# A hybrid conformer block on 8 cores: 24 of 33 token tiles transposed by DMA in place of TensorE, and adaLN gates later in the convolution stage

## The chip, the cores and the metric

One Trainium2 chip, 8 cores. Each core runs the same program on its own 2,048 tokens (and 32 tokens of halo before them); nothing is exchanged between cores. The time is the device time of the slowest core, in microseconds. The profile is of one execution, on its slowest core (core 4).

## The reference

```python
mod = silu(c) @ w_ada + b_ada                        # six vectors of 1024: shift, scale, gate, twice
h = layernorm(x) * (1 + scale1) + shift1             # (16384, 1024)
z = h @ w_in + b_in                                  # 7168 columns, split in seven
a_val, a_gate, b_gb, b_gc, b_x, g_a, g_b = split(z)
u = a_val * sigmoid(a_gate)
u = causal_depthwise_conv(u, conv_a_w, 31) + conv_a_b
u = silu(layernorm(u, ln_a_g, ln_a_b))
y_a = u @ w_a_out + b_a_out
y_b = (b_gb * causal_depthwise_conv(b_gc * b_x, conv_b_w, 3)) @ w_b_out
merged = sigmoid(g_a) * y_a + sigmoid(g_b) * y_b
x = layernorm(alpha * x + (1 + gate1) * (merged @ w_o + b_o), ln1_g, ln1_b)
h = layernorm(x) * (1 + scale2) + shift2
f = square(relu(h @ w_up + b_up))                    # 4096 columns
x = layernorm(alpha * x + (1 + gate2) * (f @ w_down + b_down), ln2_g, ln2_b)
```

Inputs and outputs are f32; the kernel multiplies in bf16.

## The kernel before

A core works on two blocks (`b` = 0, 1) of 1,024 tokens, each eight tiles of 128 tokens (`NT` = 8). Matmuls want channels on the partitions, x arrives with tokens on them. So each token tile is normalised with tokens on the partitions (`xn`, `h2n`, bf16, 128x1024), then transposed in eight 128x128 pieces into `hT` (the input of w_in) or `h2T` (the input of w_up), where the modulation `* (1 + scale) + shift` has one scalar per partition. There are 33 such tiles: the halo tile and eight of block 0's h, eight of block 1's h, and eight of h2 in each block.

The stages follow one another on TensorE: h and GLU of block 0; convolution stage of block 0 (24 steps `n_` in `token_mix`; each does a pair of projections for p, the first 16 also a piece of the 31-wide convolution); the B gate (16 steps); the merge (32 steps of two groups of eight 512-column matmuls); then GLU, convolution, gate and merge of block 1; up-projection of block 0 (64 steps of eight matmuls), down-projection, and both for block 1.

Work on other tiles is laid between these steps. `Plan` is a table from step to calls: `plan.add(n, fn, i)`; `plan.run(n)` makes them after step n. In block 0's merge it prepares block 1's h (`p1_setup`: `load`, `stats`, `root`, `norm`, `trans`). In block 1's merge it does block 0's output projection and both layer norms (`p3_setup`: `bias`, `proj`, `root1`, `ln1`, `root2`, `ln0`, `trans`), and in the up-projection of block 0 the same for block 1. The order of the calls is the order of the instructions on each engine's queue; there is no other scheduler.

`transpose_evac` does a transpose: eight TensorE transposes against an identity into banks 6 and 7 of PSUM (line 531), then one instruction per piece that applies the modulation while it reads PSUM, some on ScalarE (line 558), the rest on VectorE (line 550): four and four for block 1's h, five and three for h2. Block 0's h is transposed raw (lines 536 and 538) and modulated in place later, by `modulate` (lines 776 and 780). Matmuls rotate over the other six banks (`brot`).

`hT` has room for the halo in each of eight runs (`PW` = 132 columns, of which `NPH` = 128 are the tile's), in block 1 too; there the matmuls read `[4][128]` or `[3][128]` columns out of runs of 132 (`hcols`, `cols`).

DMAs that load weights are issued by GpSimd (they cast f32 to bf16), through a ring of four 1 MB slots (`ws_get`, `ws_release`); SP issues the loads of x, the relays of u, the stores of x1 (`ln1`) and the output. An engine waits at the head of its queue, in order.

The vectors of `mod` come from w_ada in twelve tiles of 512 columns. Tiles 4 and 5 (gate1), 6 and 7 (shift2), 8 and 9 (scale2), and 10 and 11 (gate2) are loaded two at a time into a place that two tiles share; each pair is used by 64 one-column matmuls (`ada_cols`), and only then is the next loaded. `xc0_side(n)` does this in the convolution stage of block 0: gate1 after step 2, its row (`ada_rows`, TensorE, then a DMA to `gd`) after step 3, its spread to all partitions as `g1b` after step 8, shift2 after 11, scale2 after 20. `gb0_side` uses tiles 10 and 11 after step 11 of the next stage.

Of the kernel before, what the change touches and what calls it, by code (L numbers as in the profile page):

```python
# [251 lines left out]
def build_program(needed=None):  # L252
# [1280 lines left out]
```

How the kernel before makes its waits and increments, by code:

```python
    def wait_ev(self, ev, same_ok=False):  # L63
        if ev is None:
            return
        sem, val, key = ev
        if key == self.name and (same_ok or not self.selfsync):
            return
        sid = id(sem)
        if self.seen.get(sid, 0) >= val:
            return
        self.h.wait_ge(sem, self.fw.sem_value(key, val))
        self.seen[sid] = val
# [14 lines left out]
    def mark(self, inst, reads=(), writes=()):  # L88
        self.idx += 1
        if self.fw.needs_inc(self.name, self.idx):
            self.cnt += 1
            inst.then_inc(self.sem, 1)
        ev = (self.sem, self.idx, self.name)
        for r in reads:
            r.r[self.name] = ev
        for w in writes:
            w.w = ev
            w.r = {}
        return ev
# [7 lines left out]
    def dma(self, out, in_, owner, reads=(), writes=()):  # L107
        self.deps(reads, writes)
        if owner.dsem is None:
            self.fw.nsem += 1
            owner.dsem = self.fw.nc.alloc_semaphore("d%d_%s" % (self.fw.nsem, owner.name))
        owner.dcnt += 16
        inst = self.h.dma_start(out=out, in_=in_)
        inst.then_inc(owner.dsem, 16)
        ev = (owner.dsem, owner.dcnt, "dma_" + owner.name)
        for r in reads:
            r.r["dma_%s_%d" % (owner.name, owner.dcnt)] = ev
        for w in writes:
            w.w = ev
            w.r = {}
        return ev
```

## Time and profile before

| | us |
|---|---|
| time, median of 3 runs (1172.16 to 1173.83) | 1172.42 |
| the profiled execution, its own time | 1171.64 |
| its span, slowest core; all cores 1164.0 to 1170.6 | 1170.6 |
| TensorE busy | 1100.7 |
| VectorE busy | 677.6 |
| ScalarE busy | 437.1 |
| GpSimd busy | 175.2 |

Busy times are of instructions; those of TensorE overlap at their ends, and a 512-column matmul that is listed with 379 ns follows the one before it after some 216 ns. The granted clock of TensorE is given as a share of full speed.

### The profile page before, as it was taken

To read this page: it belongs to the slowest core of one execution; us is meant where nothing else is said; L and a number is where in the kernel's file an instruction comes from. 1 tells how busy PE (TensorE), PEld (TensorE's weight loads), DVE (VectorE), ACT (ScalarE), POOL (GpSimd) and SP (SyncE) were. 2 spreads that over 40 slices of the span, in tenths; PEclk is the share of its full clock that TensorE was granted. 3 is DMA by queue.
4 is the path that set the end of the run, shared out by engine and by line. 5 is a ranking of instruction groups with operands and counts; after the bars stand their busy time and mean duration, and the time that the engine had idled before them with its cause. 6 is when DMAs were issued, how large, how long until landed. Compare 5 with 4: busy or idle time off the path is not lost.

```text
span 1170.6 us, 19292 instructions; the slowest of 8 cores (1164.0 to 1170.6 us)
## 1 busy us (share of the span) xinstructions
PE 1100.7 (94%) x6607; PEld 578.1 (49%) x6676; DVE 677.6 (58%) x1159; ACT 437.1 (37%) x773; POOL 175.2 (15%) x159
## 2 busy tenths in 40 slices
PE   1699899999999999999999999999999999999994
PEld 1366577444445677644444444444444444444441
DVE  4538576847653267588877767877032782210567
ACT  2344334844442234584466644456000043320000
POOL 4004011102100000111321021210060000004200
PEclk9999899999999999999999999999999999999998
DMA  9999959998645652398764584636944399644412
GB/s 185 180 142 124 162 90 146 166 229 169 77 73 92 111 90 35 59 180 162 127 129 92 123 157 109 130 73 141 220 72 72 73 203 240 97 73 72 73 54 90
DMA packets 150335, 143.14 MB, mean 122 GB/s; under 512 B 33840, under 2 KB 138688, under 8 KB 149984
## 3 DMA queue, kind: packets, MB, share of 16 engines
q0 software_dynamic: 106736, 87.73, 52.7%
q1 hardware_dynamic: 43504, 54.18, 16.5%
q8 instruction: 55, 0.90, 0.3%
q14 instruction: 40, 0.33, 0.1%
HBM read 203.22 MB, written 16.79 MB: 188 GB/s over the span
## 4 chain that ended last, share of the span: by engine, by line
PE 79%; DVE 8%; DMA 5%; issue 4%; ACT 3%; POOL 1%; DVEq 0%; ACTq 0%; POOLq 0%; SPq 0%
PE bank L161 78%; DMA wb<-w_in 4%; ACT nb L1063 2%; DMA wada<-w_ada 2%; DVE cbuf L1055 1%; DVE slot L500 1%; PE bank L531 1%; DVE x1r L515 1%; DVE x1r L1256 0%; DVE gt L1254 0%; DVE fT L1236 0%; ACT sg L1135 0%; DVE sg L1138 0%; DVE dg L1083 0%; DVE x L664 0%
## 5 line engine op out<-in xcount | busy, mean ns | idle before, releaser
L161 PE MATMUL bank<-hT,wb 128*128 128x512 bf16 (+4 forms) x2112 | 388.8, 337 | 1.9 <-ACT sg L1135 1.3
L161 PEld LDWEIGHTS bank<-hT,wb 128*128 128x128 bf16 x2112 | 202.7, 98 | 157.2 <-issue 14.4
L161 PE MATMUL bank<-h2T,wb 128*128 128x512 bf16 x1002 | 222.8, 379 | 3.1 <-DVE x L664 1.9
L161 PE MATMUL bank<-wb,fT 128*128 128x512 bf16 x1004 | 220.3, 379 | 1.1
L161 PEld LDWEIGHTS bank<-wb,fT 128*128 128x128 bf16 x1024 | 100.2, 98 | 120.8
L161 PEld LDWEIGHTS bank<-h2T,wb 128*128 128x128 bf16 x1024 | 99.8, 98 | 121.3 <-issue 2.9
L1234 ACT ACTIVATE rr<-bank,pvec 128x512 bf16<-128x512 f32 x128 | 85.1, 683 | 111.0 <-PE bank L161 108.9
L1236 DVE TENSOR_TENSOR fT<-rr 128x512 bf16<-128x512 bf16 x128 | 63.4, 513 | 91.0 <-ACT rr L1234 90.9
L505 ACT ACTIVATE slot<-slot,eps 128x1 f32<-128x1 f32 (+1 forms) x65 | 17.6, 291 | 253.1 <-DVE slot L502 239.1
L1254 DVE TENSOR_TENSOR gt<-bank,g2b 128x512 f32<-128x512 f32 x32 | 21.8, 682 | 121.9 <-PE bank L161 121.9
L138 POOL DMA_DIRECT2D wb<-w_in x40 | 36.3, 938 | 316.9 <-PE bank L161 296.2
L1181 ACT ACTIVATE sg<-bank,pvec 128x512 f32<-128x512 f32 x64 | 43.5, 683 | 80.1 <-PE bank L161 72.2
L903 ACT ACTIVATE sg<-bank,pvec 128x384 f32<-128x384 f32 (+3 forms) x84 | 45.3, 539 | 72.7 <-PE bank L161 69.7
L1063 ACT ACTIVATE nb<-cbuf,pvec 128x128 bf16<-128x128 f32 x128 | 63.0, 492 | 11.5 <-DVE cbuf L1055 1.3
L161 PE MATMUL bank<-v,wb 128*128 128x512 bf16 x244 | 58.8, 379 | 1.1 <-DVE v L1152 0.5
L161 PE MATMUL bank<-u,wb 128*128 128x512 bf16 x246 | 58.8, 379 | 0.5
L161 PE MATMUL bank<-wo,merged 128*128 128x512 bf16 x251 | 57.6, 379 | 0.3
L910 DVE SCALAR_TENSOR_TENSOR p<-bank,pvec,sg 128x396 bf16<-128x396 f32 (+3 forms) x48 | 27.8, 578 | 45.1 <-PE bank L161 28.7
L500 DVE BATCH_NORM_STATS2 slot<-x 128x6 f32<-128x512 f32 x64 | 44.4, 694 | 7.0 <-DVE x L517 0.5
L138 POOL DMA_DIRECT2D wb<-w_up x16 | 14.2, 890 | 223.1 <-PE bank L161 179.5
L910 DVE SCALAR_TENSOR_TENSOR u<-bank,pvec,sg 128x384 bf16<-128x384 f32 (+3 forms) x36 | 20.8, 577 | 46.3 <-PE bank L161 41.8
L997 DVE TENSOR_TENSOR wt<-wtab,cmask 128x2560 bf16<-128x2560 bf16 x32 | 47.3, 1482 | 0.0
(113 smaller groups left out, 1135.4 us busy)
## 6 DMA issues: line engine op xcount, KB each, us to landing
wb<-w_in POOLq DMA_DIRECT2D x16, 1024.0 KB, 14.3
wb<-w_up POOLq DMA_DIRECT2D x16, 1024.0 KB, 11.8
wb<-w_down POOLq DMA_DIRECT2D x16, 1024.0 KB, 8.2
wada<-w_ada POOLq DMA_DIRECT2D x12, 1024.0 KB, 18.6
wb<-w_in POOLq DMA_DIRECT2D x24, 512.0 KB, 16.6
xt<-xs SPq DMA_DIRECT2D x16, 512.0 KB, 10.0
x<-xs SPq DMA_DIRECT2D x16, 512.0 KB, 5.7
x1d<-x SPq DMA_DIRECT2D x16, 512.0 KB, 3.4
```

The lines of the kernel that those rows point to most:

```text
L138: inst = eng.h.dma_start(out=out, in_=in_)
L161: inst = pe.h.matmul(out, lhsT, rhs, start=self.first, stop=last)
L500: dve.op(lambda e: e.bn_stats(st[:npart, hh, :], src[:npart, hh * 512:(hh + 1) * 512]), reads=[rsrc, res], writes=[res])
L505: act.op(lambda e: e.activation(sl["sd"][:npart, :], sl["mv"][:npart, 1:2], AF.Sqrt, bias=eps_ap[:npart, :], scale=1.0), reads=[sl["res"], ...
L903: act.op(lambda e: e.activation(sg[k][:, 0:n], bank_ap[bi][:, 0:n], func, bias=pvec[:, PV_BIN + ca + j:PV_BIN + ca + 1 + j], scale=1.0), r ...
L910: dve.op(lambda e: e.scalar_tensor_tensor(cols(dst, j), view(bank_ap[bi2]), pvec[:, PV_BIN + cb + j:PV_BIN + cb + 1 + j], view(sg[k]), ALU ...
L997: dve.op(lambda e: e.tensor_tensor(t.rearrange("p a m (c q) -> p (a m) c q", q=R), tab, msk, ALU.mult), reads=[r_wtab, r_cmask], writes=[r ...
L1063: act.op(lambda e: e.activation(nb[:, s_, :], cbuf[:, jb, s_, :], AF.Silu, bias=pvec[:, PV_LAB + gi:PV_LAB + gi + 1], scale=pvec[:, PV_LAG ...
L1181: act.op(lambda e: e.activation(sg[k], bank_ap[bi], AF.Sigmoid, bias=pvec[:, bcol:bcol + 1], scale=1.0), reads=[bank_res[bi], r_pvec], wri ...
L1234: act.op(lambda e: e.activation(rr[k], bank_ap[bi], AF.Relu, bias=pvec[:, PV_BUP + fc:PV_BUP + fc + 1], scale=1.0), reads=[bank_res[bi], r ...
L1236: dve.op(lambda e: e.tensor_tensor(fT[:, fc, s * 512:(s + 1) * 512], rr[k], rr[k], ALU.mult), reads=[r_rr[k]], writes=[r_fT[fc][s]])
L1254: dve.op(lambda e: e.tensor_tensor(gt[t % 2], bank_ap[t], g2b[:, hs], ALU.mult), reads=[bank_res[t], r_g2], writes=[r_gt[t % 2]])
```

## The change

- `p1_setup` of block 1 and `p3_setup` of both blocks: `trans` no longer calls `transpose_evac`, but `dma_transpose`, one DMA from SP for the whole tile, from `xn` or `h2n` into `hT` or `h2T`. It waits on SP for the normalised tile and signals its own semaphore.
- The modulation is a call of its own, `mod`, over a group of tiles: three (the last time two) for block 1's h, two for h2; in place, channels chunks 0 to 4 on VectorE and 5 to 7 on ScalarE. It is planned two to four steps behind the group's last transpose.
- Block 1's `hT` is laid out without room for the halo, 1,024 columns, and its matmuls read and write contiguous columns.
- The first of the eight groups of the up-projection goes over the first 512 tokens for all four column pieces, then over the other 512.
- `xc0_side`: gate1 after step 7 (was 2), its row after 8 (3), its spread after 12 (8), shift2 after 14 (11), scale2 after 22 (20); the loads of w_ada that follow each move with them.

```diff
+    def modulate_tiles(hT, r_hT, t0, t1, sc, sh, rm):
+        for kc in range(KC):
+            view = hT[:, kc, t0 * 128:t1 * 128]
+            x_ = 0 if kc < 5 else 1
+            rw = [r_hT[t][x_] for t in range(t0, t1)]
+            if kc < 5:
+                dve.op(lambda e: e.tensor_scalar(view, view, modT[:, sc + kc:sc + kc + 1], modT[:, sh + kc:sh + kc + 1], ALU.mult, ALU.add),
+                       reads=rw + [rm], writes=rw)
+            else:
+                act.op(lambda e: e.activation(view, view, AF.Identity, bias=modT[:, sh + kc:sh + kc + 1], scale=modT[:, sc + kc:sc + kc + 1]),
+                       reads=rw + [rm], writes=rw)
+
+    def dma_transpose(dst, src, owner, reads, writes):
+        sp.deps(reads, writes)
...
+        owner.dcnt += 16
+        sp.h.dma_start(out=dst, in_=src, transpose=True).then_inc(owner.dsem, 16)
...
     def p1_setup(b, ring, xn_offs, raw, n_dve):
-        hT = sb(OFF_H[b], [128, KC, TW], BF16, "hT")
+        hT = sb(OFF_H[b], [128, KC, TW if raw else TB], BF16, "hT")
...
         def trans(i):
             npart, ri, dv = tiles[i]
+            if not raw:
+                dma_transpose(hT[:, :, i * 128:(i + 1) * 128], xn[i % nxn], own("tr%d" % (i % nxn)), [r_xn[i % nxn]], r_hT[ri])
+                return
             transpose_evac(xn[i % nxn], npart, r_xn[i % nxn], hT, r_hT[ri], dv, None if raw else (SC1, SH1, r_mod1), n_dve)
+        def mod(g):
+            modulate_tiles(hT, r_hT[1:], 3 * g, min(3 * g + 3, NT), SC1, SH1, r_mod1)
...
         def trans(t):
-            transpose_evac(h2n[t % 2], 128, r_h2n[t % 2], h2T, r_h2T[t], lambda dst, kc: dst[:, kc, t * 128:(t + 1) * 128],
-                           (SC2, SH2, r_mod2), n_dve)
+            dma_transpose(h2T[:, :, t * 128:(t + 1) * 128], h2n[t % 2], own("tr2_%d" % (t % 2)), [r_h2n[t % 2]], r_h2T[t])
+
+        def mod(i):
+            modulate_tiles(h2T, r_h2T, 2 * i, 2 * i + 2, SC2, SH2, r_mod2)
...
         def hcols(kc, s):
+            if b > 0:
+                return hT[:, kc, s * 512:(s + 1) * 512]
             return hT[:, kc, :].rearrange("p (r n) -> p r n", n=PW)[:, 4 * s:4 * s + 4, PW - NPH:PW]
...
-            for jj in range(4):
+            for jj, s in ([(jj, s) for s in range(NS) for jj in range(4)] if g == 0 else [(jj, s) for jj in range(4) for s in range(NS)]):
...
     def xc0_side(n):
-        if n == 2:
+        if n == 7:
             ada_gate(0)
-        if n == 3:
+        if n == 8:
             ada_rows(0)
-        if n == 8:
+        if n == 12:
             ada_spread(0)
-        if n in (11, 20):
-            nts, c_ = ((6, 7), SH2) if n == 11 else ((8, 9), SC2)
+        if n in (14, 22):
+            nts, c_ = ((6, 7), SH2) if n == 14 else ((8, 9), SC2)
...
-        if n in (2, 11, 20):
-            n0 = {2: 6, 11: 8, 20: 10}[n]
+        if n in (7, 14, 22):
+            n0 = {7: 6, 14: 8, 22: 10}[n]
...
-                    plan.add(9 * g + 8 + 2 * i, pp["trans"], t)
+                    plan.add(9 * g + 7 + 2 * i, pp["trans"], t)
...
+            plan.add(min(9 * g + 14, 30), pp["mod"], g)
...
-        p3_plan(pp, 2, 3, (1, 2, 4, 5, 7))
+        p3_plan(pp, 2, 3, (1, 2, 4, 5, 6), 2, 31)
...
+            if t % 2 == 1:
+                plan.add(min(n + lags[4] + mlag, last), pp["mod"], t // 2)
...
-    p3_plan(H2[1], 4, 6, (2, 4, 7, 9, 13))
+    p3_plan(H2[1], 4, 6, (2, 4, 7, 9, 11), 4, 63)
```

## Rows read from the trace of the kernel before

**Rows 1.** The page, busy time by engine (share of the span), xinstructions.
```profile
PE 1100.7 (94%) x6607; PEld 578.1 (49%) x6676; DVE 677.6 (58%) x1159; ACT 437.1 (37%) x773; POOL 175.2 (15%) x159
```
**Rows 2.** Windows by stage: window, length, busy PE PEld DVE ACT POOL, PEclk, DMA share, GB/s.
```profile
262.00:374.00 112.00, 111.53 (x579) 54.40 (x586) 62.06 (x114) 45.50 (x79) 15.48 (x14) 1.00 0.66 109
567.00:677.00 110.00, 109.42 (x548) 51.54 (x558) 85.35 (x151) 66.78 (x103) 18.74 (x14) 1.00 0.61 122
677.00:790.00 113.00, 110.53 (x534) 51.30 (x543) 84.20 (x145) 50.36 (x91) 22.42 (x14) 1.00 0.55 117
822.00:1113.00 291.00, 289.63 (x1323) 131.87 (x1348) 100.49 (x170) 46.57 (x73) 51.73 (x37) 1.00 0.64 117
```
**Rows 3.** The page, chain that ended last, share of the span by engine.
```profile
PE 79%; DVE 8%; DMA 5%; issue 4%; ACT 3%; POOL 1%; DVEq 0%; ACTq 0%; POOLq 0%; SPq 0%
```
**Rows 4.** Timeline of TensorE in block 0's merge: start, us, operation.
```profile
285.38 0.61 PE L531 MATMUL bank<-ident,xn 128*128 128x128 bf16 x8
285.83 1.89 PE L161 MATMUL bank<-hT,wb 128*128 128x512 bf16 x8
287.56 1.89 PE L161 MATMUL bank<-v,wb 128*128 128x512 bf16 x8
289.28 1.89 PE L161 MATMUL bank<-hT,wb 128*128 128x512 bf16 x8
```
**Rows 5.** Timeline of TensorE in block 0's convolution stage, [idle before <-releaser].
```profile
115.57 2.84 PE L161 MATMUL bank<-hT,wb 128*128 128x396 bf16 x16
118.25 1.29 PE L161 MATMUL bank<-ur,wt 128*128 128x128 bf16 x20
...
122.72 0.95 PE L161 MATMUL bank<-cact,wada 128*128 128x1 bf16 x32
129.13 0.99 PE L161 MATMUL bank<-cact,wada 128*128 128x1 bf16 x32 [5.46 <-DMA wada<-w_ada]
129.99 5.37 PE L161 MATMUL bank<-hT,wb 128*128 128x396 bf16 x16
135.20 1.29 PE L161 MATMUL bank<-ur,wt 128*128 128x128 bf16 x20
```
**Rows 6.** Windows around that pause, columns as in rows 2.
```profile
123.70:129.10 5.40, 0.00 (x0) 0.00 (x0) 1.17 (x1) 1.01 (x2) 0.88 (x1) 0.61 1.14 177
129.10:135.30 6.20, 6.17 (x50) 3.37 (x51) 0.34 (x2) 0.59 (x1) 0.87 (x1) 0.51 1.18 179
135.30:150.00 14.70, 14.70 (x151) 10.48 (x149) 11.78 (x17) 6.01 (x12) 0.00 (x0) 1.00 1.16 159
```
**Rows 7.** Timeline of GpSimd, 60 to 300 us: issue of tiles 4 and 5.
```profile
109.93 2.13 POOL L138 DMA_DIRECT2D wada<-w_ada  x2
```
**Rows 8.** DMA issues, 115 to 160 us: count, size, median us to landing.
```profile
wada<-w_ada POOLq DMA_DIRECT2D x2, 1024.0 KB, 26.2
```
**Rows 9.** Groups by form: busy us, mean ns | idle before, releasers.
```profile
L558 ACT ACTIVATE h2T<-bank,modT 128x128 bf16<-128x128 bf16 x80 | 36.6, 457 | 15.5 <-PE bank L531 9.5
L550 DVE TENSOR_SCALAR h2T<-bank,modT 128x128 bf16<-128x128 bf16 x48 | 16.4, 342 | 3.5
L780 ACT ACTIVATE hT<-hT,modT 128x396 bf16<-128x396 bf16 x6 | 4.3, 715 | 2.8 <-DVE modT L463 2.4
L776 DVE TENSOR_SCALAR hT<-hT,modT 128x396 bf16<-128x396 bf16 x10 | 3.8, 382 | 0.9
L776 DVE TENSOR_SCALAR hT<-hT,modT 128x264 bf16<-128x264 bf16 x5 | 1.9, 380 | 0.4
```
**Rows 10.** DMA view, 215 to 260 us: packets, hardware queue, SBUF-to-SBUF copies.
```profile
DMA packets 17565, 8.87 MB, mean 197 GB/s; under 512 B 8909, under 2 KB 16930, under 8 KB 17556
...
q1 hardware_dynamic: 9416, 4.69, 50.4%
...
u<-nb SPq DMA_DIRECT2D x26, 64.0 KB, 8.7
```
**Rows 11.** DMA issues of the whole span: store of one x1 tile.
```profile
x1d<-x SPq DMA_DIRECT2D x16, 512.0 KB, 3.4
```
**Rows 12.** Timeline in the first up-projection: TensorE behind VectorE.
```profile
768.85 3.61 PE L161 MATMUL bank<-h2T,wb 128*128 128x512 bf16 x15 [1.24 <-DVE x L664]
```

More of the change, by code:

```diff
@@ L595, in x_ring @@
         return slot, load
+    def modulate_tiles(hT, r_hT, t0, t1, sc, sh, rm):
[11 more added lines that the diff above has]
+        sp.deps(reads, writes)
+        if owner.dsem is None:
+            fw.nsem += 1
+            owner.dsem = nc.alloc_semaphore("d%d_%s" % (fw.nsem, owner.name))
+        owner.dcnt += 16
+        sp.h.dma_start(out=dst, in_=src, transpose=True).then_inc(owner.dsem, 16)
+        ev = (owner.dsem, owner.dcnt, "dma_" + owner.name)
+        for r in reads:
+            r.r["dma_%s_%d" % (owner.name, owner.dcnt)] = ev
+        for w in writes:
+            w.w = ev
+            w.r = {}
     def p1_setup(b, ring, xn_offs, raw, n_dve):
-        hT = sb(OFF_H[b], [128, KC, TW], BF16, "hT")
+        hT = sb(OFF_H[b], [128, KC, TW if raw else TB], BF16, "hT")
         _g = new_group(fw, ["hT%d_%d%s" % (b, t, ab) for t in range(NT + 1) for ab in "ab"], OFF_H[b], OFF_H[b] + HSZ)
@@ L631, in trans @@
             npart, ri, dv = tiles[i]
+            if not raw:
+                dma_transpose(hT[:, :, i * 128:(i + 1) * 128], xn[i % nxn], own("tr%d" % (i % nxn)), [r_xn[i % nxn]], r_hT[ri])
+                return
             transpose_evac(xn[i % nxn], npart, r_xn[i % nxn], hT, r_hT[ri], dv, None if raw else (SC1, SH1, r_mod1), n_dve)
-        return dict(hT=hT, r_hT=r_hT, load=load, stats=stats, root=root, norm=norm, trans=trans, n=len(tiles))
+        def mod(g):
+            modulate_tiles(hT, r_hT[1:], 3 * g, min(3 * g + 3, NT), SC1, SH1, r_mod1)
+        return dict(hT=hT, r_hT=r_hT, load=load, stats=stats, root=root, norm=norm, trans=trans, mod=mod, n=len(tiles))
     def p3_setup(b, mg, r_mg, wo, x1_offs, h2n_offs, n_dve):
@@ L863, in hcols, with hbank @@
         def hcols(kc, s):
+            if b > 0:
+                return hT[:, kc, s * 512:(s + 1) * 512]
             return hT[:, kc, :].rearrange("p (r n) -> p r n", n=PW)[:, 4 * s:4 * s + 4, PW - NPH:PW]
+        def hbank(ap):
+            return ap if b > 0 else grp4(ap)
         u = sb(OFF_U, [128, KC, TW], BF16, "u")
@@ L896, in view, with hin @@
                     return ap[:, 0:n].rearrange("p (r n) -> p r n", n=NPH)
+            def hin(kc):
+                return cols(hT, kc) if b == 0 else hT[:, kc, r0_ * 128:r1_ * 128]
             rd = hT_reads(r0_, r1_, b == 0)
@@ L900, in pair @@
             for kc in range(KC):
-                grp.mm(view(bank_ap[bi]), wa[:, kc, jj * 128:(jj + 1) * 128], cols(hT, kc), [ra[jj // 2]] + rd, last=(kc == KC - 1))
+                grp.mm(bank_ap[bi][:, 0:n], wa[:, kc, jj * 128:(jj + 1) * 128], hin(kc), [ra[jj // 2]] + rd, last=(kc == KC - 1))
             k = sg_rot.next()
@@ L908, in pair @@
             for kc in range(KC):
-                grp.mm(view(bank_ap[bi2]), wb[:, kc, jj * 128:(jj + 1) * 128], cols(hT, kc), [rb[jj // 2]] + rd, last=(kc == KC - 1))
+                grp.mm(bank_ap[bi2][:, 0:n], wb[:, kc, jj * 128:(jj + 1) * 128], hin(kc), [rb[jj // 2]] + rd, last=(kc == KC - 1))
             dve.op(lambda e: e.scalar_tensor_tensor(cols(dst, j), view(bank_ap[bi2]),
@@ L1176, in branch @@
             for kc in range(KC):
-                grp.mm(grp4(bank_ap[bi]), wt_[:, kc, jj * 128:(jj + 1) * 128], hcols(kc, s),
+                grp.mm(hbank(bank_ap[bi]), wt_[:, kc, jj * 128:(jj + 1) * 128], hcols(kc, s),
                        [rt_[0]] + hT_reads(4 * s, 4 * s + 4, False), last=(kc == KC - 1))
@@ L1223, in up @@
             wu, ru, iu = ws_get()
-            for jj in range(4):
+            for jj, s in ([(jj, s) for s in range(NS) for jj in range(4)] if g == 0 else [(jj, s) for jj in range(4) for s in range(NS)]):
                 fc = 4 * g + jj
-                for s in range(NS):
+                if True:
                     bi = brot.next()
@@ L1429, in after_gb1, with p3_plan @@
         plan.add(0, scale_wo, 15)
-        p3_plan(pp, 2, 3, (1, 2, 4, 5, 7))
-    def p3_plan(pp, first, step, lags):
+        p3_plan(pp, 2, 3, (1, 2, 4, 5, 6), 2, 31)
+    def p3_plan(pp, first, step, lags, mlag, last):
         nx = pp["nx1"]
```

4 lines of the change are left out of this document (2 added, 2 removed).

## The prediction

> **What bounds the kernel now.** The page comes first: TensorE is busy 1100.7 us, 94% of the span [rows 1]. The windows by stage come next. In each the reader is to compare TensorE's busy time with the length of the window: 111.53 of 112 us while block 0 merges, 109.42 of 110 while block 1 merges, 110.53 of 113 in the first up-projection, 289.63 of 291 behind it. VectorE reaches 85.35 of 110 and 84.20 of 113 us in the second and third, ScalarE 66.78 and 50.36, the DMA share 0.61 and 0.55 [rows 2]. The chain of waits says the same: 79% of it is TensorE [rows 3]. So in the stages where the 24 tiles are transposed, an instruction taken off TensorE shortens the end by its length, unless something new comes late. One real pause lies outside of them, in the convolution stage of block 0 [rows 5].
>
> **The change, part by part.**
>
> *Transposes leave TensorE.* The timeline shows what one tile costs: its eight transposes start at 285.38 and the next matmul at 285.83, so 0.45 us [rows 4] (the row's 0.61 us is the modelled end of a pipelined group). Sixteen matmuls behind them take 3.45 us (285.83 to 289.28), which is one step of the merge stage. 24 tiles, eight of block 1's h and sixteen of h2, are 24 x 0.445 = **10.7 us** of TensorE. They lie between saturated matmuls, so they are on the path. The 512-column matmuls that read hT and those that read v keep the same pace (1.73 us for eight, by their starts in rows 4), though hT is read there in four strided runs: making it contiguous gains nothing visible, and I cost it at nothing.
>
> *The adaLN gate moves.* At step 2 of the convolution stage TensorE does the first 32 one-column matmuls at 122.72 and then waits 5.46 us for the tile of w_ada [rows 5]. The clock's rows show what follows: granted 0.61 in the wait and 0.51 in the 6.2 us behind it, the lower of the two levels (1.2 GHz), where all else is at 1.00 [rows 6]. Sixteen matmuls of 396 columns take 135.20 - 129.99 = 5.21 us there, against 118.25 - 115.57 = 2.68 at full clock, so 2.5 us more [rows 5]. Moving the gate to step 7 asks for the tile five steps of about 3.9 us later, about 142 in the old timeline without the pause. It landed by 129.1. The wait and its slow clock go: 5.5 + 2.5 = **8.0 us**. Nothing of the moved work itself disappears (the one-column matmuls, the row, its DMA and the spread DMA on SP only run later, and the first user of g1b is bob, behind this stage).
>
> What is late next: three loads of w_ada are issued later too. Tiles 6 and 7 are now asked for at step 7 and used at step 14, seven steps or 27 us; 8 and 9 at step 14 and used at step 22, four steps of some 3.9 us and four shorter ones, about 24 us. A pair issued amid this stage's weight loads took 26.2 us to land, but it stood behind other tiles and the engines were saturated [rows 8]; the pair before was issued at 109.93 and had landed by 129.1, 19 us, and the one for 8 and 9 is issued at about 160 to 170, when the backlog is worked off [rows 7]. Cost from 0 to 3 us; I take nothing, as both covers are above 19 us.
>
> *Modulation in place.* Before, each h2 tile took five ScalarE reads of PSUM of 457 ns and three VectorE ones of 342 ns. After, a pair of tiles takes five VectorE instructions in place and three of ScalarE. The nearest rows are the same operation in place on 396 columns: 382 ns on VectorE, 715 ns on ScalarE, and 380 ns for 264 columns on VectorE [rows 9]. Over the sixteen h2 tiles VectorE goes from 48 x 0.342 = 16.4 us to 8 x 5 x 0.38 = 15.2, ScalarE from 80 x 0.457 = 36.6 to at most 8 x 3 x 0.715 = 17.2. For block 1's h, VectorE has 15 instructions of 0.38 = 5.7 us and ScalarE nine of up to 0.715 = 6.4, both less than the 8 tiles x 4 of before. Neither engine gets more work. Both stand beside TensorE, so this is worth nothing on the path. Whether it costs something depends on the wait it brings.
>
> *The new wait.* Transpose and store both issue from SP; modulation of a group waits for its last transpose at the head of VectorE and ScalarE, and behind it stand the evacuations of the banks that TensorE refills (six banks, three merge steps). Time from the normalised tile to its modulation: in block 0's merge four steps of 3.45 us, 13.8 us. In block 1's merge the transpose of tile t stands on SP behind the store of tile t+1, and two steps (about 4.6 us each with the third of a projection that falls to them) are left, 9.2 us; in the up-projection five steps of 2.3 us, 11.5 us. How long does a DMA transpose of 256 KB take? None is in this trace. From below, a 512 KB store lands in 3.4 us [rows 11]; 3.4 us is less than every cover. From above, the SBUF-to-SBUF copies of u<-nb, in rows of 256 bytes: one of 64 KB lands in 8.7 us behind its seven companions of the group [rows 10]; four of them end to end would be 35 us. As the eight of a group are together 512 KB and land in little more than one, I take 5 to 9 us for a tile. That is at or below all three covers, and a wait of 1 or 2 us is still hidden by the free banks where VectorE has room (62.06 of 112 us in block 0's merge). It has little in the up-projection, where TensorE already loses time to VectorE, as in the 1.24 us before the matmuls at 768.85 [rows 12]: 2.5 us in the window of 113, against 0.5 at the rate of the last window. VectorE's 84.2 us would then stand against 109.4 us and no longer 113. Of the eight transposes taken out there (3.6 us) I give half back, **1.8 us**; the bounds are 0 and the whole 3.6 plus the present 2 again.
>
> The order of the first up-projection group (all of one half of the tokens first) gives the last pair four groups of eight matmuls, 4 x 1.73 = 6.9 us more. No cost.
>
> *Load on the DMA engines.* 24 transposes of 256 KB. In the window with u<-nb the hardware queue's 9,416 packets took 50.4% of 16 engines over 45 us [rows 10], 38.5 ns each; 1,024 rows of 256 bytes are 39 us of one engine, or 2.5 us of all sixteen for each tile. Free are 34% of 112 us (38), 39% of 110 (43) and 45% of 113 (51) [rows 2], for eight tiles each: 4.8, 5.4 and 6.4 us a tile. So weights stay on time, at no cost. The bounds are 0 and the second rival's.
>
> The Trainium skill (VectorE: DVE Perf Modes, The three transpose paths) speaks against the change: it gives 1309 ns for a 128x128 transpose by DMA against 390 on TensorE, and advises TensorE where PSUM will do. By it a tile of eight blocks, if they run one after another, would be an estimated 10.5 us, which would lead to the first rival below; the trace shows TensorE at 0.45 us for all eight, and no DMA transpose.
>
> **Sum.** The profiled execution took 1171.6 us (span 1170.6). 1171.6 - 10.7 - 8.0 + 1.8 = 1154.7. The median of the runs, 1172.4, lies 0.8 above that execution, so **1155.5 us**.
>
> **Rivals.**
>
> *The DMA lands behind its cover* and gives the transposes' gain back: a tile takes 12 to 15 us, modulation holds VectorE, and TensorE waits for banks. For it: the 9.2 us cover and the order on SP. Against it: 8.7 us for the copies [rows 10]. Price: of 16 h2 tiles in 8 groups, each late by about 4 us with 2.5 absorbed, 8 x 1.5 = 12; so about 1164 to 1167.
>
> *The transposes fill the DMA engines* and the weights come late: slower than before. For it: the engines are 55 to 66% taken [rows 2] and the real size of a transpose's pieces isn't known. If a tile goes in pieces of 64 bytes at the same 38.5 ns, it holds all engines for 4,096 x 38.5 / 16 = 9.9 us, so eight need 79. Block 0's merge then needs 0.66 x 112 + 79 = 153 us of 112, block 1's 146 of 110, the up-projection 141 of 113: 41, 36 and 28 us too many. Three weight tiles loaded ahead, each 64 matmuls or 13.8 us long, hide 41 us in the first stage and once in the two adjacent ones: 36 + 28 - 41 = 23 us remain. With the lower clock after such pauses, as after the one at 129, two or three times 2.5: 1155.5 + 23 + 7 = 1185. It decides from about 9 us of all engines per tile on (where it costs the 17 us won). Against it: rows of 256 bytes would need only 2.5. This is also the case in which the DMA does not do what the change asks of it.
>
> *The pause only moves* to step 14 or 22 because w_ada tiles are asked for later: 8.0 us not won, 1163.5. For it: the landing of 26.2 us [rows 8] against a cover of about 24. Against it: the queue is shorter when they are issued.
>
> **How the numbers follow.** Forecast 0.62 (its own range 1151 to 1160: no give-back below, 3.6 + 2 above, and the same spread as the runs). DMA behind its cover 0.13, pause moves 0.09, DMA engines full 0.16. The range 1149 to 1170 holds the first, the third and most of the second. Changes under 0.2% (2.3 us) could not be told from none here. Faster: 0.62 + 0.09 + most of 0.13 = 0.81; same 0.04; slower 0.15.
>
> **What would show it.** Right: no 5.46 us idle for w_ada and a clock of 1.00 between 123 and 135; TensorE's matmuls fewer by 192; DMA transposes that land in 5 to 9 us; in the three stages TensorE still busy to within 1% and the windows shorter by 3.6 us each. Wrong: VectorE or ScalarE waiting for the transposing DMA, with TensorE waiting for them; a DMA share near 1 in the merge stages and TensorE waiting for wb; a new wait for w_ada at step 14 or 22; the up-projection as long as before.

## The result: slower, 1188.6 us

The changed kernel took 1188.55 us (median; the kernel before on the same chip 1172.45). Its time over that of before is 1.0113, 95% interval 1.0075 to 1.0151: slower by 1.1%, where 1155.5 was forecast. One of its four executions, 1349.49 us, had one die at a granted clock of 0.83 to 0.85; this ratio, all ratios below and the time of E8 leave such executions out. The profiled execution took 1187.17 us with a span of 1185.8, against 1171.6 and 1170.6.

The page of after first: busy time by engine, the chain by engine, the DMA packets; these answer to [rows 1, 3, 10].

```profile
PE 1099.2 (93%) x6484; PEld 568.9 (48%) x6484; DVE 675.7 (57%) x1134; ACT 408.1 (34%) x694; POOL 174.9 (15%) x159
PE 65%; DVE 13%; DMA 7%; issue 6%; ACT 5%; SPq 3%; DVEq 0%; POOL 0%; ACTq 0%; POOLq 0%
DMA packets 175676, 149.40 MB, mean 126 GB/s; under 512 B 59184, under 2 KB 164032, under 8 KB 175328
q1 hardware_dynamic: 68848, 60.48, 20.8%
```

TensorE's weight loads, one for each matmul, went from 6676 to 6484, 192 fewer as forecast (the trace of before lacks some of its matmul records). Yet its busy time fell by only 1.5 us: some matmuls ran at the low clock. The chain left TensorE (79% to 65%) for VectorE, the DMA and SP. To see where, here are windows of three stages, columns as in [rows 2], each from TensorE's first matmul of the stage to that of the next. Before (core 4): block 0's merge from its first matmul on u, block 1's merge from its first on v, the first up-projection.

```profile
255.60:361.00 105.40, 104.87 (x527) 49.51 (x536) 61.64 (x113) 43.98 (x76) 14.60 (x13) 1.00 0.65 113
537.10:677.60 140.50, 139.29 (x683) 65.03 (x696) 110.00 (x185) 77.06 (x115) 27.32 (x19) 1.00 0.61 123
677.60:822.50 144.90, 141.45 (x692) 66.04 (x705) 105.75 (x193) 71.22 (x129) 24.21 (x16) 1.00 0.58 125
```

The same stages after (core 5, the slowest):

```profile
246.90:357.40 110.50, 103.90 (x473) 46.39 (x472) 57.25 (x100) 35.76 (x53) 14.84 (x13) 0.97 0.80 135
533.40:674.00 140.60, 137.07 (x634) 61.65 (x633) 109.62 (x177) 64.73 (x84) 27.19 (x19) 1.00 0.71 126
674.00:837.80 163.80, 144.55 (x642) 63.64 (x641) 109.58 (x194) 62.43 (x103) 24.18 (x16) 0.95 0.67 129
```

Length less busy time is what TensorE stood still: 6.6, 3.5 and 19.3 us, against 0.5, 1.2 and 3.5. In the up-projection its busy time rose although 64 transposes went (50 in the records): clock 0.95. Medians over the eight cores of each stage's length serve in all that follows:

| stage, us | before | after | gates only (E1) | transposes only (E2) |
|---|---|---|---|---|
| convolution, block 0 | 90.2 | 83.2 | 83.2 | 90.1 |
| merge, block 0 | 105.4 | 108.7 | 113.9 | 102.3 |
| merge, block 1 | 140.7 | 140.6 | 140.7 | 140.6 |
| first up-projection | 144.9 | 156.7 (153.2 to 163.8) | 144.9 | 156.0 |

From the convolution stage on, every other stage is equal within 0.3 us. What lies ahead of it is not: 112.4 us before, 113.2 after, 115.2 and 115.4 in E1 and E2. The kernel before, too, took more beside the experiments, 1175.1 to 1176.3 us, so each of them is read by its ratio to that, and by its stages. Against the profiled core of before, core 5 of after has -8.4, +5.1, +0.1 and +18.9: 15.7 us, and the two executions differ by 15.5.

TensorE's timeline after has four long pauses ([idle before <-releaser]).

```profile
246.87 1.46 PE L161 MATMUL bank<-u,wb 128*128 128x512 bf16 x6
254.93 1.01 PE L161 MATMUL bank<-u,wb 128*128 128x512 bf16 x2 [6.60 <-DMA u<-nb]
...
688.34 3.57 PE L161 MATMUL bank<-h2T,wb 128*128 128x512 bf16 x8 [7.28 <-DVE h2T L603]
...
763.15 5.08 PE L161 MATMUL bank<-h2T,wb 128*128 128x512 bf16 x13 [5.33 <-DVE x L696]
...
822.46 3.80 PE L161 MATMUL bank<-h2T,wb 128*128 128x512 bf16 x10 [5.27 <-ACT rr L1276]
```

All eight cores have the third (5.3 us, at 750 to 763) and the fourth (3.8 to 5.3 us, at 808 to 822); the first two vary, up to 7.3, and are small on some cores. The windows around them give the clock.

```profile
254.90:260.00 5.10, 5.07 (x15) 1.99 (x16) 2.95 (x5) 0.61 (x1) 0.00 (x0) 0.61 0.54 169
688.40:692.30 3.90, 3.90 (x10) 1.41 (x11) 2.81 (x4) 1.98 (x5) 1.69 (x1) 0.50 1.10 341
692.30:757.80 65.50, 65.50 (x304) 29.41 (x301) 48.31 (x79) 24.85 (x41) 12.38 (x9) 1.00 0.59 128
763.20:768.90 5.70, 5.70 (x17) 2.12 (x18) 3.56 (x9) 2.08 (x4) 0.00 (x0) 0.63 0.56 92
822.50:827.00 4.50, 4.50 (x15) 1.72 (x16) 4.08 (x6) 1.55 (x3) 0.00 (x0) 0.67 0.84 159
```

Behind each pause the granted clock is 0.50 to 0.67 for 4 to 6 us, and 1.00 in the 65 us between two of them. In the up-projection of core 5: 18.9 = -3.6 (transposes) + 15.8 (standing still, 19.3 - 3.5) + 6.7, so some 2 us of slow clock for each of three pauses. The split is worked out from the windows, not measured by itself.

**The pause near 763.** Lines of the kernel: L1278 squares rr into fT, L696 adds a bank of the output projection to x, L685 is GpSimd's add of the bias bob to x, L603 modulates in place on VectorE and L606 on ScalarE, L138 issues a weight load and L615 a transpose. (Before, fT is L1236, the addition L664 and GpSimd's add L653.) All engines in time order:

```profile
756.08 1.51 SPq L615 DMA_TRANSPOSE h2T<-h2n  x1
756.64 0.92 POOL L138 DMA_DIRECT2D wb<-w_up  x1 [14.19 <-PE bank L161]
...
757.45 4.95 DVE L1278 TENSOR_TENSOR fT<-rr 128x512 bf16<-128x512 bf16 x2
757.57 4.20 POOL L685 TENSOR_TENSOR x<-x,bob 128x1024 f32<-128x1024 f32 x2
...
762.33 1.47 DVE L696 TENSOR_TENSOR x<-bank,x 128x512 f32<-128x512 f32 x2
```

Two fT instructions of 0.42 us each take 4.95: the first stands (4.62 us) until GpSimd's two adds end, and behind them stands the addition (x<-bank,x) that empties TensorE's bank. The modulation in place can suffer in the same way:

```profile
781.57 4.03 DVE L603 TENSOR_SCALAR h2T<-h2T,modT 128x256 bf16<-128x256 bf16 x3 [0.48 <-DVE h2T L603]
782.45 2.14 POOL L685 TENSOR_TENSOR x<-x,bob 128x1024 f32<-128x1024 f32 x1
```

Its form (columns: ns least/median/most) has a median of 346 ns, as estimated, but up to 3117:

```profile
L603 DVE TENSOR_SCALAR h2T<-h2T,modT x40: 339/346/3117, 596.9 to 837.6; 128x256 bf16<-128x256 bf16 x40
```

Before (core 4) the same collision is there, and TensorE lost nothing by this one:

```profile
751.31 1.48 DVE L664 TENSOR_TENSOR x<-bank,x 128x512 f32<-128x512 f32 x2
...
753.10 4.21 POOL L653 TENSOR_TENSOR x<-x,bob 128x1024 f32<-128x1024 f32 x2
...
754.62 2.99 DVE L1236 TENSOR_TENSOR fT<-rr 128x512 bf16<-128x512 bf16 x1
...
757.53 1.24 DVE L550 TENSOR_SCALAR h2T<-bank,modT 128x128 bf16<-128x128 bf16 x3
```

There one instruction lost 2.6 us. What differs is the order. Before, the addition that empties the bank (751.31) was through when the adds began (753.10). After, it stood behind two fT when they began (757.57). Its matmuls had started at 742.38 and 747.29 (wo, merged): counting the two fT at their usual 0.74 us, VectorE would have come to it 10.9 us behind them after, against 8.9 before. Over the stage fT stood still five times in each kernel, 11.9 us before and 14.0 after. L550, which reads PSUM, never took over 346 ns; the forms that stood still read and write SBUF. The Trainium skill (SBUF — State Buffer, Who interferes with whom) states this: VectorE and GpSimd share a port pair as an exclusive lock, "the other **fully blocks** (not throttle)", if VectorE's instruction has two SBUF inputs (and GpSimd's reads SBUF) or is in a 2-port mode, which tensor_scalar can enter. The trace agrees (4.95 beside 4.20 us). The rule was not weighed in the prediction.

Block 1's merge has the same pattern with a third form, the sum of the two branches:

```profile
634.01 2.81 DVE L1239 TENSOR_TENSOR merged<-tb,tb 128x512 bf16<-128x512 f32 x1
...
637.56 1.89 PE L161 MATMUL bank<-hT,wb 128*128 128x512 bf16 x8 [1.47 <-DVE x L696]
```

Its usual time is 0.69 us, a GpSimd add runs from 634.12 to 636.25, and the addition for TensorE's bank comes behind both, at 636.74. In the kernel before that addition (638.01) is ahead of the GpSimd add (639.42).

**The pauses near 688 and 822.** The waits of after (total us, times, longest) have two lines that before has not:

```profile
ACT h2T L606 <- DMA h2T<-h2n: 19.0, 2, 12.6
DVE h2T L603 <- DMA h2T<-h2n: 15.7, 2, 9.9
```

SP's and GpSimd's issues of the third case:

```profile
804.07 0.91 POOL L138 DMA_DIRECT2D wb<-w_down  x1 [19.49 <-PE bank L161]
...
804.80 1.95 SPq L615 DMA_TRANSPOSE h2T<-h2n  x1
...
817.46 2.55 DVE L603 TENSOR_SCALAR h2T<-h2T,modT 128x256 bf16<-128x256 bf16 x5 [5.79 <-DMA h2T<-h2n]
```

A weight tile of 1 MB was issued 0.7 us ahead of the transpose, and this one landed in 12.6 us. The median is in the forecast band (5 to 9 us). The first line is of all 24 transposes; the others are of the DMA view: the 16 of h2, then those issued at 756.08, 671.60 and 804.80; last column us to landing.

```profile
DMA to landing us min/median/max: 3.1/5.2/14.2
...
h2T<-h2n SPq DMA_TRANSPOSE x16, 5.2
...
h2T<-h2n SPq DMA_TRANSPOSE x1, 6.5
...
h2T<-h2n SPq DMA_TRANSPOSE x1, 14.2
...
h2T<-h2n SPq DMA_TRANSPOSE x1, 12.6
```

Over all cores: 3.1 us at best, 3.7 to 3.9 with the weights 0.9 to 1.4 us *behind* it, 6.3 to 7.1 with them 0.6 us behind (756.08), 11.5 to 12.6 with them 0.7 us in front. In block 0's merge two or three of the eight tiles took 9.5 to 13.3 us on every core, and TensorE waited for none of them: the cover was 13.8.

### The profile page after: what moved, and what is told of

Read it like the earlier page. It is cut to its first block, busy times and chain, and to the rows that moved or that the text cites. A ratio compares the mean times of both kernels' runs of the same rounds, so it can differ in the third digit from the quotient of the medians.

```text
span 1185.8 us, 18865 instructions; the slowest of 8 cores (1171.4 to 1185.8 us)
## 1 busy us (share of the span) xinstructions
PE 1099.2 (93%) x6484; PEld 568.9 (48%) x6484; DVE 675.7 (57%) x1134; ACT 408.1 (34%) x694; POOL 174.9 (15%) x159
## 3 DMA queue, kind: packets, MB, share of 16 engines
q0 software_dynamic: 106736, 87.73, 53.1%
## 4 chain that ended last, share of the span: by engine, by line
PE 65%; DVE 13%; DMA 7%; issue 6%; ACT 5%; SPq 3%; DVEq 0%; POOL 0%; ACTq 0%; POOLq 0%
PE bank L161 65%; DMA wb<-w_in 4%; DVE slot L500 3%; SPq L138 2%; DMA h2T<-h2n 2%; ACT nb L1105 2%; DVE cbuf L1097 1%; DVE x L515 1%; DVE x L517 1%; DVE h2T L603 1%; DVE x L696 1%; DVE x1r L515 1%; DMA u<-nb 1%; ACT L1223 1%; DVE x1r L1298 0%
## 5 line engine op out<-in xcount | busy, mean ns | idle before, releaser
L161 PEld LDWEIGHTS bank<-hT,wb 128*128 128x128 bf16 x2112 | 203.8, 98 | 161.3 <-issue 15.8
L161 PE MATMUL bank<-h2T,wb 128*128 128x512 bf16 x1024 | 228.7, 385 | 19.3 <-DVE h2T L603 7.3
L161 PEld LDWEIGHTS bank<-h2T,wb 128*128 128x128 bf16 x1024 | 101.0, 99 | 144.9 <-issue 28.5
L1278 DVE TENSOR_TENSOR fT<-rr 128x512 bf16<-128x512 bf16 x128 | 65.4, 530 | 89.3 <-ACT rr L1276 89.2
L138 POOL DMA_DIRECT2D wb<-w_in x40 | 36.0, 921 | 323.5 <-PE bank L161 323.2
L1105 ACT ACTIVATE nb<-cbuf,pvec 128x128 bf16<-128x128 f32 x128 | 63.0, 492 | 11.5 <-DVE cbuf L1097 1.3
L1236 DVE SCALAR_TENSOR_TENSOR tb<-bank,pvec,sg 128x512 f32<-128x512 f32 x32 | 24.0, 750 | 44.4 <-PE bank L161 30.2
## 6 DMA issues: line engine op xcount, KB each, us to landing
wb<-w_in POOLq DMA_DIRECT2D x16, 1024.0 KB, 13.8
wb<-w_in POOLq DMA_DIRECT2D x24, 512.0 KB, 19.3
```

Source lines behind the costliest of these rows:

```text
L138: inst = eng.h.dma_start(out=out, in_=in_)
L161: inst = pe.h.matmul(out, lhsT, rhs, start=self.first, stop=last)
L1105: act.op(lambda e: e.activation(nb[:, s_, :], cbuf[:, jb, s_, :], AF.Silu, bias=pvec[:, PV_LAB + gi:PV_LAB + gi + 1], scale=pvec[:, PV_LAG ...
L1236: dve.op(lambda e: e.scalar_tensor_tensor(tb_[2], bank_ap[bi2], pvec[:, PV_BAO + j:PV_BAO + j + 1], sg[k], ALU.add, ALU.mult), reads=[bank ...
L1278: dve.op(lambda e: e.tensor_tensor(fT[:, fc, s * 512:(s + 1) * 512], rr[k], rr[k], ALU.mult), reads=[r_rr[k]], writes=[r_fT[fc][s]])
```

## The experiments

A is the theory on record first in each expectation, B (and C) its rivals. Each verdict is the ratio to the kernel before in the same batch, with its 95% interval.

### E1 and E2: each half alone

E1 is the kernel before with only the gates moved (`if n == 2:` to `if n == 7:`, `(2, 11, 20)` to `(7, 14, 22)`); E2 the changed kernel with the gates at their old steps.

> The kernel before with only the adaLN calls moved (steps 7, 8, 12, 14, 22). Theory A (the pause moves): the convolution stage of block 0 takes 83.2 us instead of 91.6, but TensorE then waits 3 to 6 us for u<-nb at the start of block 0's merge, with its clock low behind it, so in all 2 to 5 us under the kernel before: 1167 to 1170. Theory B (the wait for u<-nb comes from the transposes' work): no such wait, 8 us less: 1164.

> The changed kernel with the adaLN calls where they were before. Theory A (the loss is in the first up-projection and comes from the transposes): that stage takes 153 to 164 us instead of 144.9, block 0's merge is 3 us shorter, block 1's the same; total 1180 to 1190. Theory B (the loss comes from the shifted w_ada loads): below 1172.

E1: 0.9994 (0.9983 to 1.0004), 1175.1 us. E2: 1.0114 (1.008 to 1.0149), 1189.55. A holds in both, but E1's pause is longer than A expected (3.3 to 7.6 us), and of the 2 to 5 us in all nothing is left: it wins 7.0 us in the convolution and gives all back in the merge (+8.5). TensorE of E1, core 7:

```profile
257.77 1.01 PE L161 MATMUL bank<-u,wb 128*128 128x512 bf16 x2 [7.51 <-DMA u<-nb]
```

In E2 the merge of block 0 is 3.1 us shorter than before (3.5 on the four cores that wait nowhere for u), so transposing by DMA pays there, and the old pause is back (core 5):

```profile
130.99 0.99 PE L161 MATMUL bank<-cact,wada 128*128 128x1 bf16 x32 [5.46 <-DMA wada<-w_ada]
```

### E3: the gate at step 5

```
-        if n == 2:            # before
+        if n == 5:
-        if n in (2, 11, 20):
-            n0 = {2: 6, 11: 8, 20: 10}[n]
+        if n in (5, 11, 20):
+            n0 = {5: 6, 11: 8, 20: 10}[n]
```

> The kernel before with the gate after step 5 and its row after 6, all else of adaLN where it was (spread 8, shift2 11, scale2 20). The tile of w_ada landed at 129 us, before step 5 ends. Theory A (the loads of the last tiles, moved from step 20 to 22, are what pushes u<-nb late): no wait at the merge, 8 us less than before: 1164. Theory B (any 8 us won ahead of a stage whose DMA engines are full is waited for at its end): a wait of 2 to 6 us for u<-nb, 1167 to 1170.

0.9957 (0.9942 to 0.9971), 1171.43 us; convolution 83.7, merge 106.0 with 0 to 2.9 us of wait for u left. Mostly A: three steps later is enough for w_ada, and with the other loads where they were, 5 of the 7 to 8 us are kept. The last pair of w_ada is issued 8.0 us ahead of the convolution stage's end before and in E3, 2.8 us ahead in E1 and after. ScalarE is done with nb 35.0 us behind that end in all four. The last copy of u<-nb lands at 47.9 to 50.7 before, 50.1 to 53.7 in E3, 54.1 to 59.3 in E1 and 53.1 to 57.4 after; TensorE wants it at 49.5. So the later loads delay the copies. That it is the last pair, and not the one moved from step 11 to 14, was not tested by itself.

### E4, E5 and E10: without GpSimd's adds

```
+            if not pp.get("nobias"):     # set for block 1 in E4 (on after) and E5 (on before)
                 plan.add(max(n - 2, 0), pp["bias"], t)
```

E10 takes that line out for both blocks, on after.

> The changed kernel without GpSimd's add of the bias bob to x in block 1's output projection (that add is left out of the computation). Theory A (VectorE's 2-byte SBUF-to-SBUF instructions stand still while GpSimd adds): in the first up-projection no fT or h2T instruction over 0.6 us, the pauses of 5.3 and 1.2 us behind L696 are gone; the stage is 6 to 9 us shorter, total 1178 to 1182. Theory B (VectorE is merely full): the stage is at most 2 us shorter.

> The kernel before without GpSimd's add of bob to x in block 1's output projection (left out of the computation), the control for e4. Theory A (the add stops VectorE in both kernels, but only the changed one has no room for it): the first up-projection, 144.9 us before, gets 1 to 2 us shorter here, against 13 to 20 us in the changed kernel. Theory B (the add costs each kernel the same): 8 us or more shorter here too.

> The changed kernel without GpSimd's adds of bob in both blocks (left out of the computation). Theory A (the collision also hides the transposes' gain in block 1's merge): that stage takes 137 to 138 us instead of 140.6, the first up-projection 141 as in e4. Theory B (that stage is late for another reason): 140.6.

E4: 0.998 (0.997 to 0.999), 1174.14 us; the up-projection 140.8 instead of 156.7. E5: 0.9987 (0.9976 to 0.9998); 141.7 instead of 144.9. E10: 0.9956 (0.9939 to 0.9972); 143.3 (138.2 to 148.8, by the pause at the stage's start), and block 1's merge 138.1 instead of 140.6. A in all three, though E4's gain is larger and E10's stage longer than it said. So the same adds cost the kernel before 3.2 us and the changed one 16. The window of the up-projection in E4 (core 4) against that of after above:

```profile
676.50:816.90 140.40, 138.29 (x641) 62.57 (x640) 91.39 (x189) 60.82 (x99) 7.05 (x8) 1.00 0.73 144
```

VectorE's busy time falls from 109.58 to 91.39 us with five fewer instructions: what GpSimd held is in it. Gone are the 5.33 us and, on all cores, the pause near 822 too, although the transpose behind it still lands in 11.9 to 14.6 us. That pause thus needs both, the transpose behind a weight load and a VectorE already late. The one at the stage's start stays (2.0 to 7.5 us on six cores). In block 1's merge E10's 2.5 us shows that the adds had eaten most of what transposing had won.

### E6: modulation of h2 on ScalarE alone

```
-            if kc < 5:        # VectorE, else ScalarE
+            if kc < nd:       # nd = 0 for h2
```

> The changed kernel with all eight chunks of h2's modulation on ScalarE, none on VectorE. Theory A (VectorE's in-place instructions, slow or stopped beside GpSimd's add, are what block 1's tail cannot bear): the pause of 5.3 us near 758 is gone or under 2 us, the first up-projection 6 to 10 us shorter than 163, the waits for the transposes at its start and near 817 stay; total 1178 to 1183. Theory B (the fT instructions alone collide): 159 to 163 us as before, total 1186 to 1190.

1.0157 (1.0141 to 1.0172), 1193.56 us: A fell, B is nearer. Block 1's merge does come down to 138.0, but the up-projection is 163.1. Three pauses of core 4, and one of core 0:

```profile
689.39 3.43 PE L161 MATMUL bank<-h2T,wb 128*128 128x512 bf16 x8 [4.88 <-ACT h2T L606]
756.67 10.52 PE L161 MATMUL bank<-h2T,wb 128*128 128x512 bf16 x40 [3.41 <-ACT rr L1276]
824.25 16.34 PE L161 MATMUL bank<-h2T,wb 128*128 128x512 bf16 x64 [6.91 <-ACT rr L1276]
...
755.10 6.17 PE L161 MATMUL bank<-h2T,wb 128*128 128x512 bf16 x16 [5.33 <-DVE x L696]
```

Eight ScalarE instructions of 0.6 us now stand in front of rr, which empties the banks. The pause of 5.33 us is there on seven of the eight cores, though VectorE modulates nothing of h2: it comes from fT, which waits for rr 6.0 us in front of it (core 0) and then meets the adds. So that pause is not made by a modulation that GpSimd holds, but by VectorE coming late to the adds.

### E11 and E13: the same adds in four pieces

```
-            pool.op(tensor_tensor(x1[k], x1[k], bob, ADD))
+            for q_ in range(4):
+                cs = slice(q_ * 256, (q_ + 1) * 256)
+                pool.op(tensor_tensor(x1[k][:, cs], x1[k][:, cs], bob[:, cs], ADD))
```

> The changed kernel with each add of bob cut into four instructions of 256 columns. Theory A (a VectorE instruction waits for one GpSimd instruction, and gets in between two): no fT or h2T instruction over 1.2 us, the pause of 5.3 us near 758 gone; the first up-projection 145 to 151 us. Theory B (GpSimd's queue of adds goes first whatever its pieces): VectorE stands for the whole of the adds, 4 us and more as in the changed kernel; 155 us or more.

> The kernel before with each of GpSimd's adds of bob cut in four, nothing else. Theory A (the kernel before lost its 2.7 us in the first up-projection to the same collision): that stage 141.7 us as without the add (e5), 3 us in all, ratio 0.997 to 0.998. Theory B (the added instructions cost VectorE as much as they give): no change.

E11, on after: 1.002 (1.0009 to 1.003), 1179.48 us; up-projection 149.9, merge of block 1 137.7. E13, on before: 0.9973 (0.9963 to 0.9984), 1170.46 us against 1175.14; up-projection 141.7, as with no adds at all. No work is left out, only cut. E11's timeline, core 4, at the place of the old pause:

```profile
756.67 6.42 PE L161 MATMUL bank<-h2T,wb 128*128 128x512 bf16 x29
...
759.06 2.12 DVE L1280 TENSOR_TENSOR fT<-rr 128x512 bf16<-128x512 bf16 x3
...
759.39 6.99 POOL L687 TENSOR_TENSOR x<-x,bob 128x256 f32<-128x256 f32 x8
```

VectorE now gets in between two pieces: three fT in 2.12 us, and TensorE runs on. GpSimd pays, 6.99 us instead of 4.20 for the eight pieces, which nobody waits for. The pauses for late transposes stay (1.1 to 8.1 us at the stage's start, 4.4 to 4.8 near 799 to 815). A holds in both experiments.

### E12, E7 and E9: the late transposes

E12 loads x of block 1 later, two tiles at first and then one every other step, to clear SP's queue. E7 and E9 transpose two pairs on TensorE again (the fourth of block 0, the third of block 1); E9 also at their old steps.

```
         def trans(t):
+            if t // 2 in ((3,) if b == 0 else (2,)):
+                transpose_evac(h2n[t % 2], 128, ...)      # as before
+                return
...
+                if key == "trans" and t // 2 in pp["pepairs"]:   # E9 alone
+                    lag = 7 if step == 3 else 13
```

> The changed kernel with three of the five loads of x that SP issues right behind the last transpose of block 0's h2 put off to steps 4, 6 and 8 of the up-projection. Theory A (that transpose lands after 12 to 14 us because the weight load in front and the loads behind it share the engines): it lands in 8 to 10 us, the pause at the start of the up-projection falls from 7.3 us to under 4. Theory B (what stands in front decides): 12 us or more, the pause as before.

> The changed kernel with tiles 6 and 7 of block 0's h2 and tiles 4 and 5 of block 1's transposed by TensorE as before, 20 tiles by DMA. Theory A (the two waits for a transpose of 12 to 14 us cost 7.3 and 5.3 us and the slow clock behind each): both gone, 1.8 us of transposes back, the first up-projection 10 to 15 us shorter; total 1175 to 1180. Theory B (something else would be late in their place, as VectorE is full): under 5 us shorter.

> e7 asked TensorE for its transposes one and two steps earlier than the kernel before does, and TensorE waited 5.7 us each for h2n. Here the same two pairs stay on TensorE at their old steps (7 and 13 behind the projection's). Theory A (two waits for a late transposing DMA are part of the loss): against the changed kernel's 156.7 us (median of the cores) the first up-projection takes 148 to 151, block 1's merge 141; total 1178 to 1182. Theory B (VectorE's lateness alone makes the loss): 154 us or more.

E12: 1.0122 (1.0105 to 1.0139), up-projection 156.3, the transpose in 8.0 to 14.3 us: nothing changed, so it is not what stands behind the transpose. E7: 1.0128 (1.0112 to 1.0143); it asked for the TensorE transposes before h2n was there (5.72 and 5.58 us of wait for L717 on core 4), and tells nothing of the question. E9: 1.0019 (1.0008 to 1.0029), 1178.11 us, up-projection 147.4. A: with those two pairs on TensorE the pauses at the start and near 822 are gone, and one of over 1.1 us is left (core 5, below). Block 1's merge misses the expected 141: it takes 144.1, as TensorE waits 2.3 us for h2n ahead of a transpose and has the pauses of after besides.

```profile
760.30 5.58 PE L161 MATMUL bank<-h2T,wb 128*128 128x512 bf16 x16 [5.33 <-DVE x L696]
```

### E8, E14, E15 and E16: put together

E8 is before with E3's gates and only block 1's h by DMA. E15 is E8 with the adds in quarters. E14 is E9 with the quarters and E3's gates (20 tiles by DMA); E16 is E14 with all of block 1's h2 on TensorE.

> The kernel before with the gate after step 5 (as e3) and only block 1's h (eight tiles) transposed by DMA and modulated by groups; all of h2 on TensorE as before. Theory A (the DMA transposes pay where VectorE has room and cost where it has none): block 0's merge 3.5 us shorter than in e3, all later stages as before: 3 to 4 us under e3, 0.990 to 0.994 of the kernel before. Theory B (the weights' loads delay them everywhere): not under e3.

> Gate after step 5 as in e3, adds in quarters, twenty tiles by DMA: all but tiles 6 and 7 of block 0's h2 and 4 and 5 of block 1's, which stay on TensorE at their old steps. If the three causes are the whole of the loss: block 0's merge 102 us as in e8, block 1's 138, the first up-projection 140 to 142; 12 to 15 us under the kernel before, ratio 0.987 to 0.990. If one more is hidden: above 0.992.

> Gate after step 5, adds in quarters, only block 1's h by DMA, h2 on TensorE. 8 to 11 us under the kernel before, ratio 0.991 to 0.993; behind e14 by the transposes of h2, 3 to 5 us, if those pay at all.

> As e14, but all of block 1's h2 on TensorE, 14 tiles by DMA. If DMA transposes in the first up-projection are worth their 0.45 us each once nothing collides: 2 to 3 us behind e14. If VectorE's in-place modulation there eats it: equal or ahead of e14.

| | us | ratio to before | conv. | merge 0 | merge 1 | up |
|---|---|---|---|---|---|---|
| E8 | 1169.64 | 0.9946 (0.9929 to 0.9962) | 83.7 | 102.1 | | 144.5 |
| E14 | 1158.59 | 0.9869 (0.9852 to 0.9886) | 83.2 | 102.2 | 139.6 | 139.0 |
| E15 | 1161.49 | 0.9896 (0.9881 to 0.9911) | 83.4 | 102.4 | 140.8 | 141.7 |
| E16 | 1160.61 | 0.9895 (0.9874 to 0.9917) | 83.2 | 102.1 | 139.5 | 141.7 |

Against what was expected: E8's merge of block 0 is 3.9 us shorter than E3's, as A has it, but in all it is only 0.0011 of the ratio under E3, as one core still waits for u<-nb (merge 108.5). E14 comes out just below its range (0.987 to 0.990), with block 1's merge 1.6 us longer and the up-projection at least 1 us shorter than expected. E15 is better than its range. E16 is 2.0 us behind E14, as expected, and its up-projection 2.7 us longer for six tiles on TensorE: 0.45 us a tile, the price of the forecast. E14 beats both kernels, 1.3% below before. Windows of its three stages, core 5:

```profile
247.90:350.50 102.60, 102.06 (x473) 45.91 (x472) 55.77 (x96) 35.76 (x53) 15.00 (x13) 1.00 0.81 136
526.50:666.60 140.10, 137.74 (x650) 62.59 (x649) 107.07 (x182) 69.24 (x94) 34.17 (x43) 1.00 0.75 134
666.60:805.60 139.00, 139.00 (x657) 63.53 (x656) 94.64 (x184) 62.25 (x104) 33.48 (x40) 1.00 0.67 128
```

With as many TensorE instructions in block 0's merge as the changed kernel had (x473), and 16 more in the up-projection (two tiles; 15 in the records), the first is 8 us and the last 25 us shorter than on that kernel's core 5. A transpose issued near 790 still lands in 11.6 to 14.3 us there, and TensorE does not wait.

## Why the prediction was wrong, step by step

**Transposes leave TensorE, 10.7 us: right as a term.** Block 0's merge lost 3.1 us in E2 for eight tiles (3.5 where u was not waited for; 3.6 forecast), and the up-projection reached 139.0 in E14: 144.9 - 2.7 of old pauses - six tiles of 0.445 is 139.5. The contiguous hT gained nothing, as costed.

**The adaLN gate, 8.0 us: the stretch right, "what is late next" wrong.** The convolution stage lost 7.0 to 8.4 us and runs at clock 1.00 from 123 to 135. But the step looked for the next late w_ada alone. The next late transfer was u<-nb: the moved loads and its 26 small copies meet in queues that are full (DMA share 1.24 from 200 to 247 us after, core 5), and TensorE waits up to 7.6 us (E1) with the slow clock behind it. It is the third rival with the place wrong. E1 puts it at all of the gain, E3 shows that a smaller move keeps most. So 8.0 us was a right size for the pause and a wrong one for the change.

**Modulation in place, "so this is worth nothing on the path": the step that failed.** Count and duration were right (346 ns against 380 taken; ScalarE 599 against at most 715). What failed is that a busy sum says nothing on when an instruction may run, and what comes later for it. VectorE, with a pair of tiles to modulate in one go (2.16 us at 747.78, against 1.24 for one tile before), comes some 2 us later to the addition that empties TensorE's bank. That puts GpSimd's 2.1 us adds in front of it, and fT or merged, SBUF to SBUF instructions held already before, now hold it up. Of the 2 us, 0.9 is the longer modulation; the rest is not taken apart, and E6, where ScalarE has the modulation and fT waits for it, keeps the pause. A held modulation itself (two of 40, 1.1 and 2.8 us) is the smaller part. E4 against E5 prices the collision: 15.9 against 3.2 us in the up-projection, so 12.7 us that the change made of it, of which E11 gets 6.8 back by cutting the adds. The pause near 822 is in these 12.7 and in the next term too, so the two do not add up. In block 1's merge the adds ate about 2.5 of 3.6 us (E10).

**The new wait, 5 to 9 us: the median right (5.2), its use wrong.** The cover was held against the typical landing, and it is the longest one that ends a pause: 12 to 14 us for a transpose behind a weight load. "A wait of 1 or 2 us" became two of 5 to 7 us, each with about 2 us of slow clock. The first rival described this, but priced each late group at 1.5 us and all alike; it was two groups of the eight (E9: 9.3 us of the up-projection with both back on TensorE). The estimate of 10.5 us for eight blocks one after another is refuted as a rule: all eight land in 3.1 us at best. The forecast that half of 3.6 us would be given back stands against 15.4 us (156.7 - 141.3).

**Load on the DMA engines: right.** q1's share rose by 0.208 x 1185.8 - 0.165 x 1170.6 = 53.5 us, or 2.2 for a tile (2.5 forecast), in 1,056 packets each (25,344 more over 24). The page of before has

```profile
q1 hardware_dynamic: 43504, 54.18, 16.5%
```

The rival in which the transposes fill the engines gave 1185, close to what was measured, and is nevertheless refuted, the nearness being luck: the stage shares are 0.67 to 0.80, TensorE waits nowhere for wb in these stages, and E14 is fast with 20 of the 24.

**Sum as measured,** on stage medians: -7.0 (convolution), +3.3 (merge: -3.1 won, +6.4 for u), -0.1, +11.8: +8.0; the slowest core, which sets the time, has +7 more in the up-projection, by the pause at its start.

**Open.** Why the transpose issued near 671 lands in 7 us on some cores and 14 on others, at the same distance from its weight load. That a weight load just in front is what makes a landing long fits every core and is not tested by moving that load alone. Why VectorE is 2 us late near 757 is only in part accounted for. And in E14's merge of block 1 TensorE still waits 1.4 to 2.3 us for h2n ahead of a transpose.

## What to carry to other kernels

Before an evacuation from PSUM is replaced by work in place in SBUF on VectorE, lay VectorE's queue against GpSimd's instructions in the timeline: which SBUF to SBUF instruction meets an add, and whether the one that empties a bank stands in front of it or behind it. Cutting the adds in four cost nothing and was worth 0.3% to the kernel before by itself. Hold a cover against the longest landing, not the median, and look which big load is issued just in front of it. When a pause is removed, follow the queues to the next small transfer that they delay, rather than to the next use of the moved one.

## What the runs showed of the hardware

- A DMA transpose of 128 x 1024 bf16 (256 KB) lands in 3.1 us at best, in 11.5 to 12.6 when issued 0.7 us behind a 1 MB load; SP is occupied 1.2 to 3.4 us by issuing it, against 0.33 for the plain store of an x1 tile.
- SBUF to SBUF instructions on VectorE (fT, the modulation in place, merged) stand still until GpSimd's add beside them ends: 0.42 became 2.99 us beside one add and 4.62 beside two, 0.35 up to 3.1, 0.69 up to 3.3. With the add in four pieces 0.42 became 0.94 at most (E11, core 4). The modulation that reads PSUM stayed within 346 ns.
- In the kernel after (core 5), each pause of 5 to 7 us on TensorE was followed by 4 to 6 us at clock 0.50 to 0.67.
